# Feed-forward activations turned by VectorE in blocks of 32 and SBUF-to-SBUF transfers, instead of by TensorE

## The reference

```
x += W_out(g_conv * ConformerConv(h) + g_mla * MLA(h)),  h = RMSNorm(x)
x += MemoryCrossAttention(RMSNorm(x), RMSNorm(mem))
x += square(relu(RMSNorm(x) @ w_ff1)) @ w_ff2       # w_ff1 2048 x 8192, w_ff2 8192 x 2048
return RMSNorm(x)
```

## Time and profile before

| | |
|---|---|
| median of 3 runs | 1652.18 us |
| profiled execution | 1652.81 us |
| its span | 1651.0 us |
| PE, PE weight load | 1623.5 us (98%), 1354.1 us (82%) |
| DVE, ACT | 1086.1 us (66%), 818.6 us (50%) |
| DMA | 184 GB/s from DRAM over the span |

### The profile page before, as it was taken

How to read it: one execution, slowest core, us unless ns; L and a number is a source line. 1 busy time by engine, 2 the same in 40 slices (tenths; PEclk the granted TensorE clock), 3 DMA queues, 4 the chain that set the end, 5 groups by cost and what they waited for, 6 DMA issues and landing times.

```text
span 1651.0 us, 21932 instructions
## 1 busy us (share of the span) xinstructions
PE 1623.5 (98%) x7514; PEld 1354.1 (82%) x7514; DVE 1086.1 (66%) x1469; ACT 818.6 (50%) x1067; POOL 96.3 (6%) x187
## 2 busy tenths in 40 slices
PE   8999999999999999999998999999999999999997
PEld 6888888888888888888887888888888888888885
DVE  5588888888888898655555655555555555545554
ACT  6544456555555556743445644334443444344443
POOL 8300010211111000000000000000000000000000
PEclk9999999999999999999999999999999999999998
DMA  7666655555555666557553566566656665666553
GB/s 243 196 190 185 188 159 165 171 173 177 170 161 172 215 198 186 186 183 265 176 196 115 175 183 191 191 192 181 194 189 192 189 189 187 193 189 187 181 197 119
DMA packets 159147, 304.96 MB, mean 185 GB/s; under 512 B 11593, under 2 KB 15809, under 8 KB 158657
## 3 DMA queue, kind: packets, MB, share of 16 engines
q1 hardware_dynamic: 157984, 300.45, 59.0%
q0 software_dynamic: 1056, 3.46, 0.7%
q10 hardware_dynamic: 32, 0.01, 0.0%
HBM read 301.78 MB, written 2.10 MB: 184 GB/s over the span
## 4 chain that ended last, share of the span: by engine, by line
PE 96%; ACT 1%; DVE 1%; DMA 1%; issue 0%; ACTq 0%; DVEq 0%; POOLq 0%
PE ps L1229 30%; PE ps L1231 30%; PE ps L1230 30%; PE ps L1242 2%; PE ps L1373 1%; PE ps L1372 1%; ACT hconv L726 0%; PE ps L1389 0%; DMA rows<-in_mem_dram 0%; PE ps L1383 0%; DMA x_in<-in_x_dram 0%; DVE wlo L846 0%; PE ps L1390 0%; PE ps L1352 0%; PE ps L1358 0%
## 5 line engine op out<-in xcount | busy, mean ns | idle before, releaser
L846 DVE TENSOR_TENSOR wlo<-raw,whi 128x1024 fp32r<-128x1024 f32 x561 | 686.7, 1228 | 413.5 <-ACT whi L524 408.4
L524 ACT ACTIVATE whi<-raw 128x1024 fp32r<-128x1024 f32 x561 | 591.9, 1060 | 556.4 <-PE ps L1231 545.6
L1229 PE MATMUL ps<-whi,a_hi 128*128 128x512 f32 x1248 | 493.2, 395 | 3.2 <-DVE wlo L846 2.4
L1231 PE MATMUL ps<-whi,a_lo 128*128 128x512 f32 x1248 | 486.9, 390 | 0.0
L1230 PE MATMUL ps<-wlo,a_hi 128*128 128x512 f32 x1248 | 486.6, 390 | 0.0
L1229 PE MATMUL ps<-whi,c_hi 128*128 128x512 f32 x768 | 300.0, 391 | 0.0
L1231 PE MATMUL ps<-whi,c_lo 128*128 128x512 f32 x768 | 298.9, 389 | 0.0
L1230 PE MATMUL ps<-wlo,c_hi 128*128 128x512 f32 x768 | 298.9, 389 | 0.0
L1229 PEld LDWEIGHTS ps<-whi,a_hi 128*128 128x128 f32 x1248 | 234.9, 188 | 51.5 <-issue 3.9
L1231 PEld LDWEIGHTS ps<-whi,a_lo 128*128 128x128 f32 x1248 | 234.7, 188 | 49.4
L1230 PEld LDWEIGHTS ps<-wlo,a_hi 128*128 128x128 f32 x1248 | 235.0, 188 | 47.1
(11 more groups left out here) (215 smaller groups left out, 1037.2 us busy)
## 6 DMA issues: line engine op xcount, KB each, us to landing
raw<-in_w_ff_dram SPq DMA_DIRECT2D x256, 512.0 KB, 3.9
raw<-in_w_in_dram SPq DMA_DIRECT2D x145, 512.0 KB, 3.8
raw<-in_w_mla_out_dram SPq DMA_DIRECT2D x32, 512.0 KB, 4.5
raw<-in_w_conv_out_dram SPq DMA_DIRECT2D x32, 512.0 KB, 4.3
raw<-in_w_out_dram SPq DMA_DIRECT2D x32, 512.0 KB, 4.7
raw<-in_w_ukv_dram SPq DMA_DIRECT2D x16, 512.0 KB, 3.6
raw<-in_w_xkv_dram SPq DMA_DIRECT2D x16, 512.0 KB, 4.3
raw<-in_w_uq_dram SPq DMA_DIRECT2D x16, 384.0 KB, 3.9
```

Source lines behind the costliest of these rows:

```text
L524: act.activation(whi[:, s, :], raw[:, s, :], ACT.Copy).then_inc(hi_ready, 1)
L846: dve.tensor_tensor(wlo[:, s, :], raw[:, s, :], whi[:, s, :].bitcast(F32), ALU.subtract).then_inc(lo_ready, 1)
L1229: pe.matmul(sum_, x_hi[:, k0 + k, tok], w_hi, start=(first and k == 0), stop=False)
L1231: mm = pe.matmul(sum_, x_lo[:, k0 + k, tok], w_hi, start=False, stop=(last and k == kts - 1))
```

## The change

In the feed-forward alone, PE no longer turns. After the squares of w_ff1 chunk c, DVE transposes the 32x32 blocks of each 128x512 half in place of their positions (`blocks`). The blocks then lie on the wrong quarter of the partitions; SP issues 16 transfers of 32 partitions x 1 KB (512 KB in all) from `blocks` to `moved`, behind the load of the first unit of chunk c+2. ACT and DVE make `c_hi` and `c_lo` from `moved`, one unit later in their lists than before (k = 4 for k = 3), in pieces of one token tile where it was two feature tiles; so PE waits before every second unit of the first w_ff2 chunk for both pieces of a quarter. `blocks` and `moved` lie where `xkT` to `xqT` of the cross attention lay.

```diff
+QUAD = 32
+QUADS = P // QUAD
+        blocks = at(o, "blocks", [P, QUADS, CPB, TT, QUAD])
+        moved = at(o + 4096, "moved", [P, QUADS, CPB, TT, QUAD])
+        def quads(dst, c, t):
+            return dst[:, 4 * c:4 * c + 4, P * t:P * (t + 1)].rearrange("p k (i e) -> p k i e", i=QUADS)
 # SP
+            def move_blocks(g, c):
+                sp.wait_ge(blocks_ready, g * CH + (c + 1))
+                for i in range(QUADS):
+                    for j in range(QUADS):
+                        sp.dma_start(moved[QUAD * j:QUAD * (j + 1), i, :, :, :], blocks[QUAD * i:QUAD * (i + 1), j, :, :, :]).then_inc(blocks_moved, 16)
                 for c in range(CH):
-                    load_chunk(U_FF + UPC * c, r, w_ff1, g * D + NC * c)
+                    for k in range(UPC):
+                        load(U_FF + UPC * c + k, r, w_ff1[:, 2 * k:2 * k + 2, ds(g * D + NC * c, NC)])
+                        if k == 0 and c >= 2:
+                            move_blocks(g, c - 2)
                 for c in range(CH):
                     for k in range(UPC):
                         load(U_FF + UPC * (CH + c) + k, r, w_ff2[:, ds(g * KT + 2 * k, 2), NC * c:NC * (c + 1)])
+                        if k == 0 and c < 2:
+                            move_blocks(g, c + 2)
 # ACT (the same at k = 4 of the first w_ff2 chunk, for chunk 3)
-                        if k == 3 and c:
-                            turn_out(g * CH + (T_FF + c - 1), c_hi, 4 * (c - 1))
+                        if k == 4 and c:
+                            moved_out(g, c - 1)
+            def moved_out(g, c):
+                act.wait_ge(blocks_moved, g * (16 * QUADS * QUADS * CH) + 16 * QUADS * QUADS * (c + 1))
+                for t in range(TT):
+                    act.activation(quads(c_hi, c, t), moved[:, :, :, t, :].rearrange("p i k e -> p k i e"), ACT.Copy).then_inc(turn_hi, 1)
 # DVE (moved_low in place of turn_low at k = 4, as on ACT)
+            def moved_low(g, c):
+                for t in range(TT):
+                    dve.wait_ge(turn_hi, g * (2 * CH) + (2 * (T_FF + c) + t + 1))
+                    dve.tensor_tensor(quads(c_lo, c, t), moved[:, :, :, t, :].rearrange("p i k e -> p k i e"),
+                                      quads(c_hi, c, t).bitcast(F32), ALU.subtract).then_inc(turn_lo, 1)
                     dve.tensor_tensor(rows[:, p, :, :], rows[:, p, :, :], rows[:, p, :, :], ALU.mult).then_inc(chunk_out, 1)
+                    dve.wait_ge(chunk_out, g * (2 * CH) + (N_FF + c + 1))
+                    dve.wait_ge(blocks_moved, g * (16 * QUADS * QUADS * CH) + 16 * QUADS * QUADS * c)
+                    for t in range(TT):
+                        turned_blocks = dve.transpose(blocks[:, :, :, t, :].rearrange("p j k e -> p k j e"),
+                                             rows[:, p, t, :].rearrange("p (k j e) -> p k j e", k=CPB, j=QUADS))
+                    turned_blocks.then_inc(blocks_ready, 1)
 # PE
-                        if c == CH:
-                            pe.wait_ge(turn_lo, g * (2 * CH) + (2 * splits_before(T_FF) + k + 1))
+                        if c == CH and k % 2 == 0:
+                            pe.wait_ge(turn_lo, g * (2 * CH) + (2 * splits_before(T_FF) + k + 2))
-                        if k == 3 and 1 <= c <= CH:
-                            pe.wait_ge(chunk_out, g * (2 * CH) + n)
-                            turn(None, rows[:, pair_of(n - 1), :, :], 0,
-                                 (turn_lo, g * (2 * CH) + (2 * splits_before(T_FF + c - 2) + 1)))
```

More of the change, by code:

```diff
@@ L323, in build @@
         relu_ready, fin_landed, last_rows, fin_gained = (sem(n) for n in ("relu_ready", "fin_landed", "last_rows", "fin_gained"))
+        blocks_ready, blocks_moved = sem("blocks_ready"), sem("blocks_moved")
         fin_act, fin_dve, stored = sem("fin_act"), sem("fin_dve"), sem("stored")
+        def quads(dst, c, t):
+            return dst[:, 4 * c:4 * c + 4, P * t:P * (t + 1)].rearrange("p k (i e) -> p k i e", i=QUADS)
         block = ctx.enter_context(nc.Block())
@@ L807, in ff_group @@
                             hi(U_FF + UPC * (CH + c) + k + LEAD, r)
-                        if k == 3 and c == 0:
-                            turn_out(g * CH + (T_FF + CH - 1), c_hi, 4 * (CH - 1))
+                        if k == 4 and c == 0:
+                            moved_out(g, CH - 1)
                     if last and c < CH - 1:
@@ L1174, in ff_group @@
                             reciprocal(rs_2, sd_n, R_2)
-                        if k == 3 and c:
-                            turn_low(g * CH + (T_FF + c - 1), c_lo, c_hi, 4 * (c - 1))
+                        if k == 4 and c:
+                            moved_low(g, c - 1)
                     p = pair_of(N_FF + c)
@@ L1183, in ff_group @@
                             lo(U_FF + UPC * (CH + c) + k + LEAD, r)
-                        if k == 3 and c == 0:
-                            turn_low(g * CH + (T_FF + CH - 1), c_lo, c_hi, 4 * (CH - 1))
+                        if k == 4 and c == 0:
+                            moved_low(g, CH - 1)
                         if last and k == 4 and c:
```

## The result

The changed kernel takes 1688.75 us (median of 4, 1687.28 to 1690.16) against 1652.84 us before (median of 4, 1652.05 to 1655.05): ratio 1.0214, 95% interval 1.0201 to 1.0227. I had forecast 1645 us and a range up to 1668. The way it went is rival C, SyncE's issuing, farther along than I had followed it.

The account below looks back on a forecast made before the run. PE, busy 98% of the span, bounds the kernel. Removing 16 turns gives -14.2 us, PE's stalls in w_ff2 chunks +6.8, so -7.4 from 1652.81: 1645 us; range 1638 to 1668, likeliest 1641 to 1649.

Parts of the forecast that it names:

- rival C: SP's sixteen issues become the bound: gain gone from 0.56 us apart on, 1665 us at 0.60; chance 0.27.
- Relu and squares: In the followed chunk, relu starts at 1305.28, the squares at 1306.58, and DVE is free at 1307.72.
- Block transposes: On DVE behind the squares: two of 128x512 at 0.65 us each; bounds -0.65 to +1.3 us in all.
- The later `lo`: DVE does the two `lo` behind the squares 1.3 us later; hidden from PE with 3 us to spare.
- The issues: SP issues sixteen moves behind a load, 0.44 us apart, from 1312.1 to 1318.7; bounds 0.37 and 0.60.
- Landing: A move lands 2.2 us from its issue, so all are moved at 1320.9; bounds 1.5 and 3.9.
- ACT's stand at the copies: ACT waits 3.7 us at `moved_out`, then makes two copies; DVE's second subtraction ends at 1323.0.
- What is late from that? In w_ff1 chunks nothing: After the copies, the next `hi`, relu and weight units reach PE in time, about 1.2 us to spare.
- The price of a gap: PE stands 1.7 us before unit 6 of the first w_ff2 chunk, once per group, 6.8 us in all.
- A: SP's transfers are cheap, 0.37 us or less apart, landing within 2 us: 1638 to 1640 us; chance 0.13.
- B: Slow landing of moves or dearer transposes eat the turns' gain: 1650 to 1652 us; chance 0.17.

## Why the prediction was wrong

By its own steps:

1. Relu and squares: right.
2. Block transposes: 0.69 us by row, two in 1.30. I had 0.65 each. The 1.24 us that I estimated from a figure of the Trainium skill ("VectorE: DVE Perf Modes", section "The three transpose paths") is not borne out.
3. The later `lo`: hidden, as said.
4. **The issues: this step failed.** I put 0.44 us between starts; it is 0.633, beyond my bound of 0.60. The rows were right and not of the same thing: every issue in the trace of before that I used has DRAM as its source, and with a DRAM source the very same transfers go out 0.464 apart. I had argued that fewer partitions make an issue cheaper or equal; the partitions made no difference (0.590, 0.592 and 0.594 us for 32, 64 and 128). From 0.464 to 0.633 the time goes from 1655 (one run) to 1689, so some 34 us hang on this one number. The sentence of the Trainium skill that initiating a DMA is usually small relative to the DMA ("DMA: Bandwidth & Descriptors", section "Issuing engines are not separate DMA queues") does not hold here: 0.59 us of SP against 1.9 to landing, sixteen times over.
5. Landing: 1.9 us measured, 2.2 worked out. Right, and on the safe side. The moves did go out in rows of 1 KB, 512 packets per chunk, and not in pieces of 128 bytes, which I had left open under rival C.
6. ACT's stand at the copies: place right; 6.25 to 8.16 us for 3.7, which follows from step 4.

"What is late from that? In w_ff1 chunks nothing": this was wrong even near my price. In the group that I followed in the run with DRAM as source, ACT waits up to 1.5 us for held loads (in that with twelve up to 2.0), and its last relu comes 0.6 us too late (with twelve 1.6). I had the loads land 1.73 us apart from the first landing on; in these chunks they come later than that, and 1.2 us of cover was too little to call it nothing. In the changed kernel itself each of these chunks takes 23.4 to 25.0 us for 21.76, and PE's eight waits for `wlo`, 13.4 us, come from that.

The price of a gap lacks a term. I counted a gap on PE as its width. In every run with gaps of about 2 us or more, some are followed by 5 to 12 matmul starts 0.43 us apart at a granted clock of 0.50: 1.0 to 2.4 us each time, 10.4 us in the changed kernel, where six of the twelve gaps bring it. PE at full clock had stood idle ahead of each of them. The width alone does not tell which: a gap of 1.95 us in the changed kernel is followed by slow starts, one of 2.36 there and one of 2.90 with twelve transfers are not. With the measured gaps and this term my sum near my own price becomes about +1 (-14.2 + 10.2 of gaps + 5.2 of clock, from the DRAM run) in place of -7.4; so the forecast of a gain was wrong by mechanism as well as by size.

Rival C had the place and the sign. I gave it 1665 at 0.60 and "some 1690" at 0.7; between the two, 0.633 would be about 1673, and it was 1689. Of the missing 16 us the clock is 10; the rest is in the gaps, small ones included. Rivals A and B did not happen; the packets' traffic, B's and part of C's ground, was harmless: the same 512 packets with four issues left the whole gain.

What stays open: why an SBUF source takes SP longer, why moves from GpSimd, or on two queues at once, land later than SP's alone, and what decides whether a gap is followed by the lower clock.

## What to carry to other kernels

A transfer's issue is work of the engine that issues it, in order with everything behind it: count the issues, multiply by a duration measured with the same kind of source, and look at which loads stand behind them. When a step feeds a saturated TensorE, cost a gap as its width plus the slow matmuls behind it. Where a queue's list was the bound, half of it on an idle engine was worth more than any order on one queue: it turned +36 us into -13, where all of it on the other queue left +3, as the moves landed later there.

## What the runs showed of the hardware that I had not expected

- Issue on SP's queue: 0.59 us (0.633 start to start) with an SBUF source whether for 32, 64 or 128 partitions; 0.42 (0.464) with a DRAM source of the same shape; a lone weight load 0.373.
- GpSimd issues the same transfer in 0.496 us, 0.49 from start to start, faster than SP, but it lands after 4.3 us against 1.9.
- Sixteen SBUF-to-SBUF moves split over SP and GpSimd land after 3.7 and 4.0 us.
- Behind a gap TensorE ran at 1.2 GHz for 5 to 12 matmuls, 1.0 to 2.4 us lost, in a stage whose clock is otherwise 1.00; gaps as short as 1.95 us did it, and one of 2.90 did not.
